# Middle buffers 128 bytes lower, the second token tile's last pieces by column halves, and two low-rank products issued alternately

## What is computed

```python
for i in range(DEPTH):                       # DEPTH = 2
    hn = rmsnorm(h, pre_mix_g[i])
    proj = hn @ (nsa_w_in if i == 0 else rwkv_w_in)
    prim = nsa_mixer(...) if i == 0 else rwkv7_time_mix(...)
    mix = jnp.concatenate([prim, memory_attention(...)], axis=-1) @ w_out[i]
    h = h + rmsnorm(mix, post_mix_g[i])
    hn = rmsnorm(h, pre_ffn_g[i])
    gu = hn @ w_ffn_in[i]
    ff = (silu(gu[..., :FFN_HIDDEN]) * gu[..., FFN_HIDDEN:]) @ w_ffn_out[i]
    h = h + rmsnorm(ff, post_ffn_g[i])
```

## Time and profile before

| | us |
|---|---|
| median of 3 runs | 773.31 |
| lowest and highest run | 771.53, 773.51 |
| profiled execution | 773.02 |
| its span | 771.3 |
| what lies around the span | 1.7 |

### The profile page before, as it was taken

How to read it: one execution, slowest core, us unless ns; L and a number is a source line. 1 busy time by engine, 2 the same in 40 slices (tenths; PEclk the granted TensorE clock), 3 DMA queues, 4 the chain that set the end, 5 groups by cost and what they waited for, 6 DMA issues and landing times.

```text
span 771.3 us, 15179 instructions
## 1 busy us (share of the span) xinstructions
PE 741.0 (96%) x6549; PEld 637.6 (83%) x6549; DVE 445.2 (58%) x645; ACT 393.8 (51%) x654; POOL 106.6 (14%) x163
## 2 busy tenths in 40 slices
PE   4999998999999999999999999999899999999996
PEld 4789975688888888888888878999788888888885
DVE  4777787647766566433252738533657756656423
ACT  5744766647645555413465436523248554555311
POOL 8120066600000000000300046500000000000000
PEclk9999989999999999999999999999999999999999
DMA  9846710026656555565733430000046565645511
GB/s 303 311 141 212 256 51 2 2 82 222 205 174 200 182 189 193 177 204 164 226 115 110 133 134 11 4 4 4 3 153 202 179 204 169 211 167 209 172 54 56
DMA packets 78277, 111.71 MB, mean 145 GB/s; under 512 B 2124, under 2 KB 64738, under 8 KB 78210
## 3 DMA queue, kind: packets, MB, share of 16 engines
q1 hardware_dynamic: 77090, 107.67, 41.9%
q0 software_dynamic: 976, 3.04, 1.3%
q10 hardware_dynamic: 144, 0.04, 0.0%
HBM read 109.68 MB, written 1.05 MB: 144 GB/s over the span
## 4 chain that ended last, share of the span: by engine, by line
PE 90%; DVE 4%; ACT 3%; DMA 1%; issue 1%; POOL 0%; DVEq 0%; SPq 0%; ACTq 0%
PE ps L1026 19%; PE ps L1188 11%; PE ps L726 11%; PE ps L728 10%; PE ps L727 10%; PE ps L1029 10%; PE ps L1014 8%; PE ps L760 2%; PE ps L846 1%; PE ps L895 1%; PE ps L869 1%; DMA hn<-mem 1%; ACT scores L1412 1%; DVE row_max L1897 1%; PE ps L816 1%
## 5 line engine op out<-in xcount | busy, mean ns | idle before, releaser
L1826 DVE TENSOR_TENSOR w_lo<-w_raw,w_hi 128x2048 fp32r<-128x2048 f32 (+2 forms) x90 | 202.1, 2259 | 83.1 <-ACT w_hi L1360 83.1
L1026 PE MATMUL ps<-x_hi_lo,w_hi 128*128 128x512 f32 x640 | 201.2, 396 | 0.0
L1360 ACT ACTIVATE w_hi<-w_raw 128x2048 fp32r<-128x2048 f32 (+2 forms) x90 | 167.9, 1885 | 38.6 <-PE ps L728 37.2
L1029 PEld LDWEIGHTS ps<-x_hi_lo,w_lo 128*128 128x128 f32 x640 | 120.2, 188 | 28.4
L1029 PE MATMUL ps<-x_hi_lo,w_lo 128*128 128x256 f32 x640 | 125.7, 278 | 0.0
L1026 PEld LDWEIGHTS ps<-x_hi_lo,w_hi 128*128 128x128 f32 x640 | 97.4, 189 | 0.0
L726 PE MATMUL ps<-w_hi,x_hi_lo 128*128 128x512 f32 (+3 forms) x208 | 73.9, 355 | 2.8 <-DVE x_hi_lo L2047 2.0
L728 PE MATMUL ps<-w_hi,x_hi_lo 128*128 128x512 f32 (+3 forms) x208 | 71.9, 346 | 0.0
L727 PE MATMUL ps<-w_lo,x_hi_lo 128*128 128x512 f32 (+3 forms) x208 | 71.9, 346 | 0.0
L726 PE MATMUL ps<-w_hi,hidden_hi 128*128 128x512 f32 x176 | 69.5, 395 | 0.0
L728 PE MATMUL ps<-w_hi,hidden_lo 128*128 128x512 f32 x176 | 69.5, 395 | 0.0
(11 more groups left out here) (365 smaller groups left out, 1018.7 us busy)
## 6 DMA issues: line engine op xcount, KB each, us to landing
w_raw<-w_ffn_in SPq DMA_DIRECT2D x44, 1024.0 KB, 5.1
w_raw<-w_ffn_out SPq DMA_DIRECT2D x22, 1024.0 KB, 5.0
w_raw<-rwkv_w_in SPq DMA_DIRECT2D x11, 1024.0 KB, 5.4
w_raw<-w_out SPq DMA_DIRECT2D x8, 1024.0 KB, 5.1
w_raw<-nsa_w_in SPq DMA_DIRECT2D x6, 1024.0 KB, 14.3
w_raw<-w_mem_kv SPq DMA_DIRECT2D x2, 1024.0 KB, 8.9
w_raw<-nsa_cmp_k_w SPq DMA_DIRECT2D x2, 1024.0 KB, 5.4
w_raw<-nsa_cmp_v_w SPq DMA_DIRECT2D x2, 1024.0 KB, 5.4
```

Of the source, the lines that this page charges most:

```text
L1026: pe.matmul(psum[:, bank + j, :], kt_of(w_hi, i, k)[:, cols[j]], xx[:, k, :, :].rearrange("p c n -> p (c n)"), start=k == 0, stop=False)
L1029: ins = pe.matmul(psum[:, bank + j, 0:SEQ], kt_of(w_lo, i, k)[:, cols[j]], xh[:, k, :], start=False, stop=k == KD - 1)
L1360: act.activation(w_hi[:, i % SPL, 0:size(i)], raw[:, i % RAW, 0:size(i)], ACT.Copy).then_inc(hi_done, 1)
L1826: dve.tensor_tensor(w_lo[:, i % RAW, 0:size(i)], raw[:, i % RAW, 0:size(i)], w_hi[:, i % SPL, 0:size(i)], ALU.subtract).then_inc(lo_done, 1)
```

## The change

**Buffers.** `colM` (26 columns of f32, 104 bytes, rounded to 128) is taken out of the `put` sequence and set near the end of the memory. Every buffer behind it, from `consts` on, comes to lie 128 bytes lower. `PH` becomes 138,496, which is 256 bytes past a multiple of 512. `w_lo`, `w_hi`, `w_raw`, `h`, `x_hi_lo` and `hn` stay.

**Column halves.** In `full_gemm` the last pieces of tile 1 (all four for m = 0 and 2, three for m = 1 and 3) are run for column half 0 first, all of them, which is then counted in the new semaphore `p_half`, and then for half 1, where each counts in `used`. The number of matmuls is the same, and so is the place of `norm_tile(m, 0)`. ACT squares half 0 of tile 1 (`first_squares(m, 1)`) and DVE multiplies it by the gain (`first_half(m, 1)`) ahead of the copies of tile 0; the rest of `post(m, 1)` stays behind them.

**Low-rank products.** The products of decay and rate are issued in turn, for each block of 128 features first the one and then the other. The wait for `fm_out` stands ahead of the second pair of both.

```diff
-        colM = put("one_minus_mu_ka", [P, 26])
...
+        colM = at(ROOM // 32 * 32 - 128, "one_minus_mu_ka", [P, 26])
...
+        TAIL = (4, 3)
...
+                tail = [j for j, t in order if t and (last, 1) in order][-TAIL[m % 2]:]
                 for j, t in order:
+                    if t and j in tail:
+                        continue
...
                     for nh in range(2):
-                        if (j, t) == (last, 1) and nh and m < 3:
-                            norm_tile(m, 0)
...
+                        ins = half_piece(j, t, nh)
                     if t == TT - 1:
                         ins.then_inc(used, 1)
                     elif j == last:
                         ins.then_inc(p_acc, 1)
+                for j in tail:
+                    ins = half_piece(j, 1, 0)
+                if tail:
+                    ins.then_inc(p_half, 1)
+                for j in tail:
+                    if j == last and m < 3:
+                        norm_tile(m, 0)
+                    half_piece(j, 1, 1).then_inc(used, 1)
...
-            def lora_pair(j, bank, rows, src, done):
+            def lora_pairs(j, banks):
                 for i in range(2):
                     f = 2 * j + i
...
+                    for bank, rows, done in zip(banks, (slice(0, LORA), slice(LORA, P)), (z_mm, a_mm)):
+                        ins = pe.matmul(psum[:, bank, i * SEQ:(i + 1) * SEQ], lora[rows, f * P:(f + 1) * P], wg[rows, 0, :],
+                                        start=True, stop=True)
+                        if i == 1:
+                            ins.then_inc(done, 1)
...
-            for j in range(FT // 2):
-                lora_pair(j, j, slice(0, LORA), wg[0:LORA, 0, :], z_mm)
             for j in range(FT // 2):
                 if j == 1:
                     pe.wait_ge(fm_out, 2)
-                lora_pair(j, (3, 6, 7)[j], slice(LORA, P), wg[LORA:P, 0, :], a_mm)
+                lora_pairs(j, (j, (3, 6, 7)[j]))
...
+            def first_squares(m, t):
+                act.wait_ge((p_acc, p_half)[t], m + 1)
+                a, b = acc_bank(m, t), turn_bank(m, t)
+                act.activation(psum[:, b, :], psum[:, a, :], ACT.Square, accum_out=psum2[:, t, 0:1]).then_inc(p_sq, 1)
...
+            def gained(m, t, i):
+                dve.tensor_tensor(hn[:, t, HALVES[i]], psum[:, acc_bank(m, t) + i, :], gain[:, HALVES[i]], ALU.mult).then_inc(p_tmp, 1)
...
+            def first_half(m, t):
+                n = TT * m + t
+                dve.wait_ge(p_sq, 2 * n + 1)
+                gained(m, t, 0)
+                dve.tensor_scalar(pbias[:, t:t + 1], psum2[:, t, 0:1], 1.0 / D, EPS, ALU.mult, ALU.add).then_inc(p_bias, 1)
...
             def post(m, t, last_piece):
...
-                    dve.wait_ge(used, last_piece)
...
+                    dve.wait_ge(p_sq, 2 * n + 2)
+                    gained(m, t, 1)
...
                     if t == 0:
                         split_to(last_piece + 2)
+                        first_half(m, 1)
                     tile_lo(m, t)
```

More of the change, by code:

```diff
@@ L347, in trunk @@
             sem("p_acc"), sem("p_sq"), sem("p_tmp"), sem("p_rms"), sem("p_h"))
-        p_bias, j_tp, j_hi, j_lo = sem("p_bias"), sem("tile_turned"), sem("tile_hi"), sem("tile_lo")
+        p_bias, p_half, j_tp, j_hi, j_lo = sem("p_bias"), sem("p_first_half"), sem("tile_turned"), sem("tile_hi"), sem("tile_lo")
         f_mm, f_ev, f_tp = sem("tok_strip"), sem("tok_strip_out"), sem("strip_turned")
@@ L987, in full_gemm, with half_piece @@
                 pairs = range(n) if m % 2 else OUT_PAIRS[m // 2]
+                def half_piece(j, t, nh):
+                    for k in range(2):
+                        kk = 2 * pairs[j] + k
+                        c = slice(512 * nh, 512 * nh + 512)
+                        ins = three(psum[:, acc_bank(m, t) + nh, :], ah[:, kk, t * P:(t + 1) * P],
+                                    al[:, kk, t * P:(t + 1) * P], kt_of(w_hi, i0 + j, k)[:, c],
+                                    kt_of(w_lo, i0 + j, k)[:, c], start=j + k == 0,
+                                    stop=j == last and k == 1)
+                    return ins
+                tail = [j for j, t in order if t and (last, 1) in order][-TAIL[m % 2]:]
                 for j, t in order:
+                    if t and j in tail:
+                        continue
                     if t == 0:
@@ L1111, in strip_turns @@
                 ins.then_inc(f_tp, 1)
-            def lora_pair(j, bank, rows, src, done):
+            def lora_pairs(j, banks):
                 for i in range(2):
                     f = 2 * j + i
-                    ins = pe.matmul(psum[:, bank, i * SEQ:(i + 1) * SEQ], lora[rows, f * P:(f + 1) * P], src, start=True, stop=True)
-                ins.then_inc(done, 1)
+                    for bank, rows, done in zip(banks, (slice(0, LORA), slice(LORA, P)), (z_mm, a_mm)):
[3 more added lines that the diff above has]
+                            ins.then_inc(done, 1)
             def memory_step(s):
@@ L1530, in join @@
                         split_to(last_piece + 2)
+                        first_squares(m, 1)
                     tile_hi(m, t)
@@ L1804, in _ @@
             for t in range(TT):
+                if t:
+                    first_squares(3, t)
                 post(3, t, first["down", 1] + N_DOWN)
@@ L2385, in _ @@
             for t in range(TT):
+                if t:
+                    first_half(3, t)
                 post(3, t, first["down", 1] + N_DOWN)
```

16 lines of the change are left out of this document (6 added, 10 removed).

## The result

The changed kernel takes 768.0 us, median of 4 runs (767.42 to 769.43), beside 773.41 us for the kernel before (4 runs, 771.53 to 773.85). The ratio is 0.9945 with a 95% interval of 0.9932 to 0.9959: faster by 0.55%. Its profiled execution took 768.51 us with a span of 766.8, 4.5 us under the span of before.

The account below looks back on a forecast made before the run. PE was taken to bound the kernel, busy 741.0 of 771.3 us and 90% of the chain that ended last. 773.0 - 3.0 - 0.8 + 0.5 + 0 - 0.4 = 769.3 us, range 767.6 to 773.2.

Parts of the forecast that it names:

- Address, -3.0: Down projections: with buffers 128 bytes lower, 528 matmuls start 0.2267 instead of 0.2324 us apart, 3.0 us less.
- one at a loss: Down projections: the new offset is worse, matmuls 0.2381 us apart, +3.0 us, time 775.3; chance 10%.
- rival A: Down projections: the address makes no difference, the 5.7 ns belong to something else; time 772.3; chance 20%.
- Low-rank products, -0.8: Decay and rate products issued in turn: 24 matmuls overlap better, less a wait behind the first 8; 0.8 us gained.
- bound of 1.8 us: Low-rank products: largest gain, if pairs cost only the longer of the two and the wait were gone.
- Joins 0 and 2, +0.25 each: Later piece release delays ACT's weight piece and tile 0's strips, mostly regained at tile 1's turn; +0.25 us each.
- Rival D: Address works, but the joins' strip delay goes through in full (+1.7) and alternation gives nothing; 771.3; chance 8%.
- Join 1, 0: Join 1: `hn` of tile 1 comes some 0.4 us earlier, but PE's strips hide it; gain 0.
- the end, -0.4: Join 3, at the kernel's end: reciprocal, `h` and the stores come 0.4 us earlier, with nothing hiding it.

Follow-up runs that it names:

- the last kernel: Changed kernel with last three pieces by column halves in all joins and the low-rank `fm_out` wait cut in two; 765.16 us, ratio 0.9905 to before.

## Why the prediction was right

The forecast was 769.3 us, faster; 768.0 was measured, inside the 767.6 to 773.2 of the range, though only 0.4 us above its lower end. The mechanisms that it named came true; one stretch of the kernel that changed was not in it. Point by point:

- **Address, -3.0.** Right in size: 528 x 5.7 ns = 3.0, and 1.5 us in each down projection. The reason given, a distance to the weights with a common factor of 256 bytes, was right, but it was a guess from one good and one bad value, given with a rival at no effect and one at a loss; the runs behind it removed the doubt. The Trainium skill, page "SBUF — State Buffer", section "SBUF: two separate sides", gives weight loads a second, independent read port. The conclusion that the prediction set beside rival A, that the stationary buffer's address would then not matter, did not come true. The measurement decides: 0.2267 against 0.2324 us per matmul by a shift of the buffers.
- **Low-rank products, -0.8.** Measured -0.96. The mechanism was right in both halves, the wait behind 8 matmuls included (0.59 us). The size was 0.16 us too cautious: 16 matmuls took 390.96 - 389.03 = 1.93 us, where the forecast gave them 2.14 from the rate in the earlier trace rows, which contains a start-up. Its bound of 1.8 us does not follow from the words beside it: half of 4.62 us would be 2.3. The kernel without a gap gained 1.82.
- **Joins 0 and 2, +0.25 each.** Measured +0.28 each. The step that could have gone wrong, how much of DVE's delay comes through, was worked out row by row and, counted from the turn of tile 0, held: ACT's weight piece 1.4 us later (1.42), copies of tile 0 1.2 us later (1.06), strips 0.85 us later (0.85, 3.10 against 2.25), no wait at the turn of tile 1 (none). Rival D, the delay in full, is excluded by the 0.65 us that come back at the turn.
- **Join 1, 0, and the end, -0.4.** Both as forecast; the reciprocal starts 0.79 us after the product, where 0.75 was written.
- **What it did not have.** The sum of the terms measured is -3.8 (forecast -3.7). The other 0.7 us between the two profiled executions are +0.3 up to 110 us and -1.0 in the chunk phase. The first varies from execution to execution, by -1.5 to +1.5 us against before over the thirteen profiled ones. The second does not lie outside the edit: the buffers that PE reads there lie 128 bytes lower too, and the prediction put them at nothing without a row for it. The medians fit a gain there (4.0 us for the buffer moved alone, where the down projections give 3.0), but its cause is open (last section). That the median came out 1.3 us below the forecast is thus not accounted for by the terms of the sum, and that the range held it is in part luck.

## What to carry to other kernels

Read PE's timeline as distances between starts, and compare stages of equal shape: a busy share of 96% hid 5.7 ns in each of 528 matmuls, and the remedy was to place the stationary buffer at a multiple of 256 bytes from the moving weights. Look for it in the spacing first: another product of this kernel did not mind 128 bytes. Where work is reordered so that one consumer gets its data earlier, look at what the same reordering releases later, and keep the piece that another engine wants at once out of it: with three pieces instead of four the same idea went from +0.28 to -0.65 us in each of two joins. Take a wait for only as much as the next instruction needs; set for the whole, it cost 0.86 us here.

## What was not expected of the hardware

**Distance between operands.** For 128x512 matmuls with a new stationary operand each, the spacing was 0.2267 us at a distance of 0 modulo 256 bytes, 0.2333 at 64, 0.2324 to 0.2333 at 128 and 0.2288 at 192. At 0 the starts repeat at 227, 227, 226 ns; in the kernel before they go round in a cycle of seven from 228 to 241 ns. The mean difference of 5.7 ns is thus a pattern of several sizes, not a matmul that is longer each time. Its origin is open.

**Small stalls of PE in the chunk phase.** Between 523 and 543 us the profiled execution of before has four stalls of PE of 0.19 to 0.27 us, where the one of after has a single stall of 0.28 us. They stand 128 matmuls apart or a multiple of it, give or take one. The chain that ended last breaks there: before, then after (start us, length us, what):

```profile
511.54 11.60 PE ps L1188 x374
...
523.20 3.94 PE ps L1188 x127
```
```profile
510.00 19.77 PE ps L1204 x665
```

In the kernel with only the low-rank part such stalls stand earlier, six of them between 472 and 500 us. Laid side by side over all thirteen profiled executions, they are not spread evenly. From the matmul that starts at 486.05 us in before to the one at 549.24 it takes 63.2 us in before, 62.8 with the column halves alone and with the low-rank products alone, and 62.7 with all buffers up by 128: these are the four kernels in which `PH` is 384 past a multiple of 512 from the weights. It takes 63.5 with `PH` up by 64, 62.3 with `PH` up by 192, and 62.1 in all seven others, after and the kernel with only the buffer moved among them. So about 1 us may well come with the place of the buffers. The rule of 256 bytes is not it, since `PH` up by 256 has the distance of before and takes 62.1. Nor do the stalls follow the place alone: they vary from 62.7 to 63.2 within the four, and the kernel with only the buffer moved has one of 0.33 us at 469 us. With one profiled execution of each kernel the cause stays open. What they are worth is more than two of the terms of this prediction.

**The granted clock in the attention.** PE's granted clock falls once in this stretch, whose instructions no edit touches, but not at the same time in each execution, and in one of the thirteen (`x_hi_lo` up by 128) it stays at 1.00. Columns as above, first before, then the last kernel:

```profile
94.00:98.00 4.00, 4.00 (x57) 3.75 (x56) 3.46 (x14) 2.96 (x8) 0.18 (x1) 1.00 0.50 163
98.00:102.00 4.00, 4.00 (x23) 2.71 (x22) 3.25 (x14) 2.02 (x8) 3.71 (x7) 0.51 0.29 99
```
```profile
98.00:102.00 4.00, 2.76 (x20) 1.58 (x18) 3.68 (x13) 2.34 (x9) 4.00 (x7) 1.00 0.19 69
...
106.00:110.00 4.00, 4.00 (x23) 2.81 (x21) 1.64 (x6) 2.05 (x10) 1.82 (x2) 0.50 0.02 4
```

Before has 1.2 GHz (0.51) from 98 us on, straight behind four us with PE busy throughout at 2.4 GHz; the last kernel still has 2.4 GHz there, with PE busy for 2.76 of 4 us, and is at 1.2 GHz (0.50) in 106 to 110 us, where before is back at 2.4. The kernels with only the buffer moved and with only the low-rank products fall late too (0.50 in 106 to 110 us). The same 507 matmuls, from 98.5 us to the output projection, take 69.6 to 69.7 us in these three executions, 67.9 in before and 67.6 in the one without a fall; that the later fall is what costs the 2 us is argued and not shown. A single execution of this kernel therefore carries differences of one to two microseconds that no edit explains, and terms under a microsecond are better read in the stage where they arise than in the total.
